# Low parts of attention's second weight pair: from VectorE's norm to GpSimd

## The chip, the cores and the metric

The kernel runs on one core of one Trainium2 chip (trn2). The metric is the device time of one execution in microseconds (us). Three runs of the kernel before gave 2669.30, 2670.77 and 2672.90 us, a median of 2670.77 us. The time of the kernel after is compared with it.

## What is computed

Two model blocks stand one behind the other, on a sequence of 512 positions and a width of 1024, all in 32-bit floats. The first has an S5 state-space mixer, a feed-forward layer, a short convolution and another feed-forward layer, and ends with `rms_norm(x, final_g)`. The second has dilated window attention, a feed-forward layer, an HGRN2 mixer and a last feed-forward layer. The stretch of this study lies between the two:

```
    return rms_norm(x, final_g)                     # end of the first block
...
    proj = (x @ w_in).reshape(B, S, N_GROUPS, 3, ATTN_HEADS, ATTN_HEAD_DIM)
    # start of dilated_attention_mixer: w_in is 1024 x 9216
```

`rms_norm` divides each position's 1024 numbers by the root of their mean square and multiplies by a gain; attention projects the result with `w_in` to queries, keys and values.

## The kernel before, in words

**Split products.** A product of 32-bit accuracy is made of three passes of TensorE over reduced operands. Each operand is the sum of a high part (rounded to the type fp32r) and a low part (operand less high part). Activations stand as `Hh` and `Hl`, or `Gh` and `Gl`; weights as `Wh` and `Wl`, and in attention as `WhA` and `WlA`. A tile is `Wh*Hl + Wl*Hh + Wh*Hh`, three matmuls for each of eight slices k of the contraction.

**The weight stream.** Weights come as `pairs`, numbered by p; each pair has two halves h. SP loads half h of pair p from HBM into `raw[:, h]`; ScalarE casts it to the high part (`split_half`, L1169 to L1177, or `split`) and raises `split_h`; VectorE subtracts, giving the low part (`low_half`, L1613 to L1616, or `low`), and raises `split_l`. `raw` has one buffer for each half, so SP's load of pair p waits for `split_l >= 2p - 1 + h` (L472): the low part of the same half of the pair before must be done. TensorE waits for `split_l >= 2p + 2` before it uses pair p. In attention a half is 128 x 1536; there are 24 pairs from P_ATTN on, in two buffers (`wa[p % 2]`).

**The norm in front of attention** is number 4. Its input X is complete only when the last product of the feed-forward layer is (`last_product`), and it is done in two halves of 256 columns (positions), so that TensorE can start on the first half while the second is normed. For each half VectorE adds the squares, TensorE sums them over partitions, ScalarE takes a first estimate of the reciprocal root, VectorE betters it in three steps (`newton`, L1624 to L1626), and then for each slice k VectorE multiplies (`scaled`, L1968), ScalarE casts to `Hh` (L1192) and VectorE subtracts to `Hl` (`lowp`, L2009), raising `nm_l`. TensorE's first three attention tiles (L808 to L810) take slice k of a half as soon as its `nm_l` is there: nine matmuls of 256 columns for each k and half, 72 for a half. Only then do the next tiles (L800 to L802, from pair P_ATTN + 1) follow.

**The order around the change** is written out by hand in each engine's program. ScalarE (`norm`, L1204 to L1221) casts half 0 of pair P_ATTN + 1 behind slices 4 and 5 of the first half, then makes the estimate for the second half, casts slices 6 and 7, and then casts half 1 of the pair. VectorE (`last_down`, L2042 to L2102) ends the first half's slices 6 and 7, computes the low part of half 0 of pair P_ATTN + 1, and only then does the three `newton` steps of the second half (`rstd_end`). It does slices 0 to 3 of the second half, computes the low part of the pair's half 1, and does slices 4 to 7.

GpSimd works at the start (tables of the state-space mixer, L2463 to L2532) and issues 42 loads for the modulation weights, the last 40 each behind a wait for VectorE's use of the buffer (L2546 to L2548). It has nothing behind them in its program.

Of the kernel before, what the change touches and what calls it, by code (L numbers as in the profile page):

```python
# [17 lines left out]
F32 = mybir.dt.float32  # L18
# [31 lines left out]
P_ATTN = P_FFN_B + 17  # L50
# [29 lines left out]
def half(h):  # L80
    return slice(h * H2, (h + 1) * H2)
# [7 lines left out]
def tiles_done(n, k, h):  # L89

    f = first_halved(n)
    before = 0 if n == 1 else 10 + 12 * (n - 2)
    return before + (k + 1 if k < f else f + h * (KT - f) + k - f + 1)
# [26 lines left out]
def half_width(p):  # L120

    if P_CONV <= p < P_CONVO:
        return (4 * 384, 4 * 384)
    if P_ATTN <= p < P_ATTNO:
        return (4 * 384, 4 * 384)
    if P_HGRN <= p < P_HGRNO:
        return (2048, 2048) if p in (P_HGRN, P_HGRNO - 1) else (1024, 1024)
    if p in (P_FFN_A + 15, P_FFN_A + 16, P_FFN_B + 15, P_FFN_B + 16):
        return (2048, 1024)
    return (2048, 2048)  # L130


def build(nc, xT, xU, cT, cC, adap, adaw, bada, norms, s5a, s5bc, s5d, wstream, convw, lnp, hgn, lbl,
          rot, masks, hmask, consts, jsel, gsel, out):
    with ExitStack() as ctx:
        masks = masks.bitcast(BF16)

        def sem(name):
            return ctx.enter_context(nc.semaphore(name))

        def sb(name, shape, dt=F32, c=ctx):
            return c.enter_context(nc.sbuf_tensor(name, shape, dt))
# [20 lines left out]
        raw = sb("raw", [P, 2, HALF])  # L163
# [119 lines left out]
        ada2_used, c2_in, c2_act = sem("ada2_used"), sem("c2_in"), sem("c2_act")  # L283
        split_h = sem("split_h")
        split_l = sem("split_l")
        acc_ready = sem("acc_ready")
        free_act = sem("free_act")
        free_dve = sem("free_dve")
# [20 lines left out]
        class Order:  # L309
# [4 lines left out]
            def step(self, ins):  # L314
                ins.then_inc(self.s, 1)
                self.n += 1

            def sync(self):
                self.eng.wait_ge(self.s, self.n)

            def link(self, ins):
                self.step(ins)
                self.sync()
# [41 lines left out]
        def w_high(p, h, n):  # L365
            return w_part(Wh, WhA, p, h, n)

        def w_low(p, h, n):
            return w_part(Wl, WlA, p, h, n)
# [1230 lines left out]
        def _(dve):  # L1600
# [12 lines left out]
            def low_half(p, h):  # L1613
                dve.wait_ge(split_h, 2 * p + h + 1)
                w = half_width(p)[h]
                TT(w_low(p, h, w), raw[:, h, 0:w], w_high(p, h, w).bitcast(F32), ALU.subtract).then_inc(split_l, 1)  # L1616

            def ahead(p):
                if p + 1 < N_PAIRS:
                    low(p + 1, half_width(p + 1))  # L1620
# [12 lines left out]
            n, r, q, m, s = pr[12], pr[13], pr[14], pr[15], pr[7]  # L1633
# [238 lines left out]
            def add_square(n, k, h=0):  # L1872

                f = first_halved(n)
                c = slice(0, T) if k < f else half(h)
                dve.wait_ge(nm_sq, squares_done(n, k, h))
                if k > 1:
                    dve.wait_ge(nm_sa, square_adds_done(n, k - 1, h))
                TT(SQA[:, c], SQA[:, c], sq[:, k % 2, c], ALU.add).then_inc(nm_sa, 1)

            for j in range(4):
                p = P_SSM + j
# [76 lines left out]
            def scaled(n, k, h):  # L1959
                gain, bias, eps = NORM[n]  # L1960
                c = half(h)
                t = tmp[:, k % 4, c]
                if n in LN_INDEX:
                    if k >= AHEAD:
                        link(TT(t, X[:, k, c], mu[:, c], ALU.subtract))
                    STT(t, t, gain(k), Rn[:, c], ALU.mult, ALU.mult).then_inc(nm_t, 1)
                elif bias is None:
                    STT(X[:, k, c], X[:, k, c], gain(k), Rn[:, c], ALU.mult, ALU.mult).then_inc(nm_t, 1)  # L1968
                else:
                    STT(t, X[:, k, c], gain(k), Rn[:, c], ALU.mult, ALU.mult).then_inc(nm_t, 1)  # L1970

            def last_pair(k):

                c = half(0)
                t = tmp[:, k % 4:k % 4 + 2, c]
                if k >= 4:
                    dve.wait_ge(nm_l, normed_done(8, k - 3, 0))
                    link(TT(t, X[:, k:k + 2, c], twice(mu[:, c]), ALU.subtract))
                TT(t, t, twice(Rn[:, c]), ALU.mult).then_inc(nm_t, 2)
# [23 lines left out]
            def lowp(n, k, h):  # L2003
                gain, bias, eps = NORM[n]
                c = half(h)
                hh = Hh[:, k, :].bitcast(F32)
                dve.wait_ge(nm_h, normed_done(n, k, h))
                if bias is None:
                    TT(class_half(Hl[:, k, :], h), X[:, k, c].rearrange("p (n r) -> p n r", r=4), class_half(hh, h), ALU.subtract).then_inc(nm_l, 1)  # L2009
                else:  # L2010
                    STT(Hl[:, k, c], tmp[:, k % 4, c], bias(k), hh[:, c], ALU.add, ALU.subtract).then_inc(nm_l, 1)

            def normed(n, h, ks):

                for k in ks:
                    if n == 8:
                        if k % 2 == 0:
                            last_pair(k)
                        continue
                    if k == 0:  # L2020
                        scaled(n, 0, h)
                    if k + 1 < KT:
                        scaled(n, k + 1, h)
                    lowp(n, k, h)
# [17 lines left out]
            def last_down(p, n, add):  # L2042

                ln = LN_INDEX.get(n)

                def tiles(k, h):
                    c = half(h)
                    if k == 6 and h == 1:
                        add_square(n, 4, 1)
                        add_square(n, 5, 1)  # L2050
                    if k == 4 and h == 0:
                        for x in range(1, 4):
                            add_square(n, x)
                    if h:
                        dve.wait_ge(acc_ready, 4 * p + k - 2)
                    else:
                        dve.wait_ge(acc_half, 2 * (n - 1) + k // 2 - 1)
                    add(k, PS[:, 4 * (p % 2) + 2 * h + k // 2 - 2, :].rearrange("p (m n) -> p m n", m=2), c)
                    if ln is not None:
                        for x in (k, k + 1) if k == 4 else (k,):  # L2060
                            dve.wait_ge(nm_x, tiles_done(n, x, h))
                            sync()
                            ins = TT(nv[:, 0, c], nv[:, 0, c], X[:, x, c], ALU.add)
                            if n == 8 and h == 1 and x == KT - 2:
                                link(ins)
                                STT(nv[:, 0, c], nv[:, 0, c], -1.0, X[:, KT - 1, c], ALU.mult, ALU.subtract).then_inc(nm_xs, 1)
                            elif x < KT - 2:
                                step(ins)
                            else:
                                ins.then_inc(nm_xs, 1)  # L2070
                    if k == 4 and h == 0:
                        add_square(n, 4, 0)
                        add_square(n, 5, 0)
                    if k == 6:
                        add_square(n, 6, h)

                ahead(p)
                tiles(4, 0)
                tiles(6, 0)
                rstd(n, 0)  # L2080
                normed(n, 0, (0, 1))
                tiles(4, 1)
                normed(n, 0, (2, 3))
                tiles(6, 1)
                dve.wait_ge(nm_x, tiles_done(n, 7, 1))
                dve.sem_inc(free_dve, 1)
                if n == 4:
                    normed(n, 0, (4, 5))
                    rstd(n, 1, early=True)
                    normed(n, 0, (6, 7))  # L2090
                    low_half(P_ATTN + 1, 0)
                    rstd_end(n, 1)
                else:
                    normed(n, 0, range(4, KT))
                    if n == 8:
                        last_half()
                        return
                    rstd(n, 1)
                normed(n, 1, range(4))
                if n == 4:  # L2100
                    low_half(P_ATTN + 1, 1)
                normed(n, 1, range(4, KT))  # L2102

            hc = [10, 0]

# [123 lines left out]
            for j in range(8):  # L2229
                p = P_CONV + j  # L2230
# [68 lines left out]
            for un in range(8):  # L2299
                p = P_ATTN + 3 * un  # L2300
# [140 lines left out]
        def _(pool):  # L2441
# [103 lines left out]
            for a in range(len(ADA2)):  # L2545
                if a >= 2:  # L2546
                    pool.wait_ge(ada2_used, a - 1)
                pool.dma_start(adab[:, a % 2, :], adaw[ADA2[a] - N_ADA_PE]).then_inc(ada2_in[a % 2], 16)  # L2548


def layout(x, c, norm1_g, norm2_g, w_ada, b_ada, ssm_a_re, ssm_a_im, ssm_log_step, ssm_b_re, ssm_b_im, ssm_c_re, ssm_c_im,
           ssm_d, ssm_w_out, conv_w_in, conv_w, conv_w_out, w_ffn_in, w_ffn_out, final_g, attn_w_in_2, attn_w_out_2,
# [156 lines left out]
```

## Time and profile before

| what | value |
|---|---|
| median of three runs | 2670.77 us |
| the profiled execution's own time | 2671.11 us |
| its span | 2669.3 us |
| VectorE busy | 1467.4 us, 55% |
| ScalarE busy | 1050.7 us, 39% |
| GpSimd busy | 116.7 us, 4% |
| mean granted clock of TensorE | 0.994 of full speed |

A busy time is the sum of an engine's instructions; overlaps between engines aren't taken out. The span is the profiled part of the execution; 1.8 us of the execution lie around it. All times inside the trace count from the start of the span.

### The profile page before, as it was taken

To read this page: it belongs to the slowest core of one execution; us is meant where nothing else is said; L and a number is where in the kernel's file an instruction comes from. 1 tells how busy PE (TensorE), PEld (TensorE's weight loads), DVE (VectorE), ACT (ScalarE), POOL (GpSimd) and SP (SyncE) were. 2 spreads that over 40 slices of the span, in tenths; PEclk is the share of its full clock that TensorE was granted. 3 is DMA by queue.
4 is the path that set the end of the run, shared out by engine and by line. 5 is a ranking of instruction groups with operands and counts; after the bars stand their busy time and mean duration, and the time that the engine had idled before them with its cause. 6 is when DMAs were issued, how large, how long until landed. Compare 5 with 4: busy or idle time off the path is not lost.

```text
span 2669.3 us, 38086 instructions
## 1 busy us (share of the span) xinstructions
PE 2625.1 (98%) x15920; PEld 2217.9 (83%) x15920; DVE 1467.4 (55%) x2173; ACT 1050.7 (39%) x1495; POOL 116.7 (4%) x150
## 2 busy tenths in 40 slices
PE   6999999999999999999999999999999999999998
PEld 3689888888898888888888888988888988988887
DVE  8967555565563333465555555744336777833335
ACT  4535222233242222355555555523223665522323
POOL 7610000000000000000000000000000000000000
PEclk8999999999999999999999999999999999999999
DMA  6084555422322322222222222132222222232220
GB/s 244 2 307 169 194 190 189 181 72 95 111 95 97 104 103 100 87 72 77 79 72 72 78 78 81 56 125 95 95 95 80 60 84 95 80 111 95 95 95 32
DMA packets 46246, 282.89 MB, mean 106 GB/s; under 512 B 6129, under 2 KB 8561, under 8 KB 20098
## 3 DMA queue, kind: packets, MB, share of 16 engines
q1 hardware_dynamic: 40146, 238.02, 26.1%
q0 software_dynamic: 5936, 42.51, 4.2%
q8 instruction: 125, 2.05, 0.3%
q14 instruction: 39, 0.32, 0.0%
HBM read 278.41 MB, written 2.10 MB: 105 GB/s over the span
## 4 chain that ended last, share of the span: by engine, by line
PE 89%; DVE 7%; ACT 3%; DMA 1%; issue 1%; SPq 0%; DVEq 0%; ACTq 0%
PE PS L665 18%; PE PS L666 18%; PE PS L667 18%; PE PS L800 4%; PE PS L802 4%; PE PS L801 4%; PE PS L889 2%; PE PS L757 1%; PE PS L758 1%; PE PS L756 1%; PE PS L637 1%; PE PS L829 1%; PE PS L830 1%; PE PS L831 1%; PE PS L877 1%; PE PS L691 1%
## 5 line engine op out<-in xcount | busy, mean ns | idle before, releaser
L665 PE MATMUL PS<-Hl,Wh 128*128 128x512 f32 x1256 | 489.1, 389 | 0.8 <-DVE Wl L1611 0.7
L666 PE MATMUL PS<-Hh,Wl 128*128 128x512 f32 x1256 | 488.7, 389 | 0.0
L667 PE MATMUL PS<-Hh,Wh 128*128 128x512 f32 x1256 | 488.7, 389 | 0.0
L1167 ACT CAST Wh<-raw 128x2048 fp32r<-128x2048 f32 (+2 forms) x156 | 281.3, 1848 | 400.5 <-PE PS L667 380.3
L1611 DVE TENSOR_TENSOR Wl<-raw,Wh 128x2048 fp32r<-128x2048 f32 (+2 forms) x160 | 347.0, 2207 | 67.0 <-ACT Wh L1167 66.8
L665 PE MATMUL PS<-Gl,Wh 128*128 128x512 f32 x880 | 342.5, 389 | 0.0
L666 PE MATMUL PS<-Gh,Wl 128*128 128x512 f32 x880 | 342.4, 389 | 0.0
L667 PE MATMUL PS<-Gh,Wh 128*128 128x512 f32 x880 | 342.4, 389 | 0.0
L665 PEld LDWEIGHTS PS<-Hl,Wh 128*128 128x128 f32 x1256 | 235.8, 188 | 50.1 <-DVE Wl L1611 1.4
L667 PEld LDWEIGHTS PS<-Hh,Wh 128*128 128x128 f32 x1256 | 235.8, 188 | 49.1
L666 PEld LDWEIGHTS PS<-Hh,Wl 128*128 128x128 f32 x1256 | 235.8, 188 | 48.6
L667 PEld LDWEIGHTS PS<-Gh,Wh 128*128 128x128 f32 x880 | 165.2, 188 | 34.4
L665 PEld LDWEIGHTS PS<-Gl,Wh 128*128 128x128 f32 x880 | 165.2, 188 | 34.3
L666 PEld LDWEIGHTS PS<-Gh,Wl 128*128 128x128 f32 x880 | 165.2, 188 | 34.1
L1365 ACT ACTIVATE tmp<-PS 128x512 f32<-128x512 f32 x108 | 64.6, 598 | 314.4 <-PE PS L667 311.6
L800 PE MATMUL PS<-Hl,WhA 128*128 128x512 f32 x424 | 170.2, 402 | 0.0
L802 PE MATMUL PS<-Hh,WhA 128*128 128x512 f32 x424 | 165.6, 391 | 0.0
L801 PE MATMUL PS<-Hh,WlA 128*128 128x512 f32 x424 | 165.3, 390 | 0.0
L2116 DVE TENSOR_TENSOR tmp<-PS,tmp 128x512 f32<-128x512 f32 x44 | 30.4, 691 | 244.9 <-PE PS L667 240.2
L1371 ACT CAST Gh<-tmp 128x512 fp32r<-128x512 f32 x108 | 62.8, 620 | 216.7 <-DVE tmp L2116 214.4
L756 PE MATMUL PS<-Gl,Wh 128*128 128x256 f32 x480 | 137.3, 286 | 0.0
L2213 DVE TENSOR_TENSOR tmp<-tmp 128x512 f32<-128x512 f32 x64 | 43.6, 690 | 169.6 <-ACT tmp L1365 169.6
(460 smaller groups left out, 4790.5 us busy)
## 6 DMA issues: line engine op xcount, KB each, us to landing
raw<-wstream SPq DMA_DIRECT2D x152, 1024.0 KB, 6.5
raw<-wstream SPq DMA_DIRECT2D x64, 768.0 KB, 4.5
adab<-adaw POOLq DMA_DIRECT2D x40, 1024.0 KB, 5.7
raw<-wstream SPq DMA_DIRECT2D x20, 512.0 KB, 3.7
raw<-adap SPq DMA_DIRECT2D x4, 1024.0 KB, 11.2
ada_land<-adap SPq DMA_DIRECT2D x4, 1024.0 KB, 19.2
X<-xT SPq DMA_DIRECT2D x1, 2048.0 KB, 8.7
XU<-xU SPq DMA_DIRECT2D x1, 1536.0 KB, 15.3
```

Source lines behind the costliest of these rows:

```text
L665: mm(o, Wh[:, s, c0:c0 + P], xl[:, k, :], start=k == 0, stop=False)
L666: mm(o, Wl[:, s, c0:c0 + P], xh[:, k, :], start=False, stop=False)
L667: last = mm(o, Wh[:, s, c0:c0 + P], xh[:, k, :], start=False, stop=k == kt - 1)
L756: mm(o, Wh[:, s, c0:c0 + P], Gl[:, k, c], start=k == 0, stop=False)
L800: mm(o, WhA[p % 2][:, c0:c0 + P], Hl[:, k, :], start=k == 0, stop=False)
L801: mm(o, WlA[p % 2][:, c0:c0 + P], Hh[:, k, :], start=False, stop=False)
L802: return mm(o, WhA[p % 2][:, c0:c0 + P], Hh[:, k, :], start=False, stop=k == KT - 1)
L889: return mm(PS[64 * h:64 * h + 64, 7 if (un, r) == (7, 3) else 6, r * P + lo:r * P + hi], v[:, 64 * h:64 * h + 64], PT[h][:, j * P + lo:j ...
L1167: nc.scalar.copy(w_high(p, h, widths[h]), raw[:, h, 0:widths[h]]).then_inc(split_h, 1)
L1365: A(tmp[:, t % 4, :], PS[:, 4 * (p % 2) + m, :], func).then_inc(hid_t, 1)
L1371: nc.scalar.copy(Gh[:, g0 + m, :], tmp[:, t % 4, :]).then_inc(hid_h, 1)
L1611: TT(w_low(p, h, widths[h]), raw[:, h, 0:widths[h]], w, ALU.subtract).then_inc(split_l, 1)
```

## The change

GpSimd computes the two low parts of pair P_ATTN + 1. It raises a new semaphore `split_p`. VectorE no longer computes them; it waits for `split_p` and raises `split_l` itself, for half 0 behind slices 0 to 3 of the second half of the norm, and for half 1 behind slices 4 to 7.

```diff
+        split_p = sem("split_p")
...
                     normed(n, 0, (6, 7))
-                    low_half(P_ATTN + 1, 0)
                     rstd_end(n, 1)
...
                 normed(n, 1, range(4))
                 if n == 4:
-                    low_half(P_ATTN + 1, 1)
+                    dve.wait_ge(split_p, 1)
+                    dve.sem_inc(split_l, 1)
                 normed(n, 1, range(4, KT))
+                if n == 4:
+                    dve.wait_ge(split_p, 2)
+                    dve.sem_inc(split_l, 1)
...
                 pool.dma_start(adab[:, a % 2, :], adaw[ADA2[a] - N_ADA_PE]).then_inc(ada2_in[a % 2], 16)
+
+            for h in range(2):
+                p = P_ATTN + 1
+                w = half_width(p)[h]
+                pool.wait_ge(split_h, 2 * p + h + 1)
+                TTg(w_low(p, h, w), raw[:, h, 0:w], w_high(p, h, w).bitcast(F32), ALU.subtract).then_inc(split_p, 1)
```

`TTg` is GpSimd's `tensor_tensor`. The operands and the result are those of the removed instructions.

## Rows read from the trace of the kernel before

**Rows 1.** The page: busy time of TensorE, and the chain that ended last
```profile
PE 2625.1 (98%) x15920; PEld 2217.9 (83%) x15920; DVE 1467.4 (55%) x2173; ACT 1050.7 (39%) x1495; POOL 116.7 (4%) x150
...
PE 89%; DVE 7%; ACT 3%; DMA 1%; issue 1%; SPq 0%; DVEq 0%; ACTq 0%
```

**Rows 2.** Waits of TensorE, whole run: us in total, times, longest us
```profile
PE PS L808 <- DVE Hl L2009: 3.8, 2, 2.9
```

**Rows 3.** Timeline of TensorE in norm 4: start, us, instruction, idle before
```profile
1143.01 0.39 PE L808 MATMUL PS<-Hl,WhA 128*128 128x256 f32 x1 [0.91 <-DVE Hl L2009]
...
1145.14 0.28 PE L810 MATMUL PS<-Hh,WhA 128*128 128x256 f32 x1
1148.28 0.58 PE L808 MATMUL PS<-Hl,WhA 128*128 128x256 f32 x1 [2.85 <-DVE Hl L2009]
...
1154.19 0.28 PE L808 MATMUL PS<-Hl,WhA 128*128 128x256 f32 x1
...
1159.59 0.40 PE L800 MATMUL PS<-Hl,WhA 128*128 128x512 f32 x1
```

**Rows 4.** Stretches: length, TensorE busy (instructions), granted clock, DMA share, GB/s
```profile
1148.00:1150.00 2.00, 1.72 (x8) 0.50 0.46 190
```

**Rows 5.** Timeline of VectorE, same stretch
```profile
1140.80 0.48 DVE L1968 SCALAR_TENSOR_TENSOR X<-X,NRM,Rn 128x256 f32<-128x256 f32 x1
1142.35 1.15 DVE L2009 TENSOR_TENSOR Hl<-X,Hh 128x256 fp32r<-128x256 f32 x2 [1.06 <-ACT Hh L1192]
1143.40 1.75 DVE L1616 TENSOR_TENSOR WlA<-raw,WhA 128x1536 fp32r<-128x1536 f32 x1
1145.07 0.42 DVE L1624 TENSOR_TENSOR nv<-Rn 128x256 f32<-128x256 f32 x1
...
1147.62 0.60 DVE L2009 TENSOR_TENSOR Hl<-X,Hh 128x256 fp32r<-128x256 f32 x1 [0.30 <-ACT Hh L1192]
...
1150.90 1.75 DVE L1616 TENSOR_TENSOR WlA<-raw,WhA 128x1536 fp32r<-128x1536 f32 x1
```

**Rows 6.** Timeline of ScalarE: the two casts of pair P_ATTN + 1, and the next pair's
```profile
1139.38 1.50 ACT L1177 CAST WhA<-raw 128x1536 fp32r<-128x1536 f32 x1
...
1142.56 1.48 ACT L1177 CAST WhA<-raw 128x1536 fp32r<-128x1536 f32 x1
...
1166.19 1.49 ACT L1177 CAST WhA<-raw 128x1536 fp32r<-128x1536 f32 x1
```

**Rows 7.** Timeline of GpSimd: two inputs of three sizes, VectorE not in its way
```profile
21.87 0.46 POOL L2471 TENSOR_TENSOR AP_<-etmp 128x128 f32<-128x128 f32 x1
...
25.64 0.66 POOL L2471 TENSOR_TENSOR QP<-etmp 128x224 f32<-128x224 f32 x1
...
41.19 1.27 POOL L2532 TENSOR_TENSOR Et<-etmp 128x512 f32<-128x512 f32 x1
```

**Rows 8.** Timeline of VectorE while GpSimd works
```profile
27.09 1.59 DVE L1770 TENSOR_TENSOR rt<-QP,BC 128x512 f32<-128x512 f32 x1
28.71 0.69 DVE L1774 TENSOR_TENSOR Ft<-PS,rt 128x512 f32<-128x512 f32 x1
...
36.13 1.26 DVE L1769 TENSOR_TENSOR PS<-QP,BC 128x512 f32<-128x512 f32 x1
37.31 1.75 DVE L1770 TENSOR_TENSOR rt<-QP,BC 128x512 f32<-128x512 f32 x1
```

**Rows 9.** Timeline of GpSimd in the same two stretches
```profile
26.48 1.65 POOL L2506 TENSOR_TENSOR ftmp<-QP,BC 128x512 f32<-128x512 f32 x1 [0.18 <-POOL QP L2471]
28.21 1.43 POOL L2507 TENSOR_TENSOR ftmp<-QP,BC 128x512 f32<-128x512 f32 x1
...
35.78 1.06 POOL L2525 TENSOR_TENSOR etmp<-AP_,BC 128x512 f32<-128x512 f32 x1
36.92 1.59 POOL L2529 TENSOR_TENSOR Et<-etmp 128x512 f32<-128x512 f32 x1
```

**Rows 10.** Weight loads: SP's queue in norm 4, and us from issue to landing
```profile
1145.32 62.54 SPq L473 DMA_DIRECT2D raw<-wstream  x8
```
```profile
raw<-wstream SPq DMA_DIRECT2D x64, 768.0 KB, 4.5
```

## The prediction

> **What bounds the kernel now.** I began with the page. TensorE is busy for 98% of the span, and the chain that ended last is 89% TensorE [rows 1], so time is lost or won only where TensorE stands still. Next I read whom it waits for: in norm 4 it waits for VectorE's `Hl`, 3.8 us in two waits [rows 2]. The timeline of TensorE places them. It is 0.91 us idle before slice 6 of the first half. After slice 7, whose last matmul begins at 1145.14, it is 2.85 us idle until slice 0 of the second half at 1148.28 [rows 3]. The wait has an aftermath: the granted clock is then 0.50, which is 1.2 GHz [rows 4]. The 27 matmuls from 1148.28 to 1154.19 take 5.91 us; the other 45 of the half, from 1154.19 to 1159.59, take 5.40 us, or 0.120 us each at 2.4 GHz. At that rate 27 would take 3.24 us, so the low clock costs 2.67 us.
>
> The timeline of VectorE says why TensorE waits. Its two `Hl` of slices 6 and 7 end at 1143.50. The low part of weight half 0 fills 1143.40 to 1145.07, where `newton` begins, and the first `Hl` of the second half ends at 1147.62 + 0.60 = 1148.22 [rows 5]. The removed instruction thus lies on the path for 1145.07 - 1143.40 = 1.67 us. From the start of `newton` to that `Hl` are 3.15 us. The other low part, at 1150.90, costs TensorE nothing now: it works on slices 0 to 3 until about 1155.
>
> **Part 1: two instructions leave VectorE.** By itself, the first brings `newton` and TensorE's restart forward by 1.67 us. The second shortens VectorE's queue by as much, but slice 4 waits for nothing in it while TensorE is at the low clock, so I take 0. If the clock stayed high, slice 4 would be wanted 36 matmuls, 4.3 us, behind slice 0, and the low part would start to show; its removal then keeps that cover.
>
> **Part 2: the same work on GpSimd.** With two inputs it takes 0.46 us for 128 columns, 0.66 for 224 and 1.27 for 512 [rows 7]. That is (1.27 - 0.46) / 384 = 0.0021 us a column. For 1536 columns: 1.27 + 1024 x 0.0021 = 3.43 us each, 6.9 us for both. No row shows GpSimd writing fp32r. As bounds I take VectorE's 1.67 us below and, above, twice the reckoned 3.43; I choose 3.43, since the removed instruction shows VectorE's own pace unchanged by that type. GpSimd can begin when ScalarE's casts end, at 1139.38 + 1.50 = 1140.88 and 1142.56 + 1.48 = 1144.04 [rows 6].
>
> **Part 3: what it does to VectorE.** This term decides. While GpSimd works early in the kernel, VectorE's instructions with both inputs in SBUF are held up: 1.59 us, 1.26 and 1.75 for 128x512. The one that takes an input from PSUM, at 28.71, runs in its 0.69 us [rows 8]. The ends fit a hold until GpSimd is done. GpSimd's instruction of 26.48 ends at 28.13, and VectorE's of 27.09 ends at 28.68, 0.55 us later; GpSimd's of 35.78 ends at 36.84, and VectorE's of 36.13 ends at 37.39, again 0.55 us later. GpSimd is held up in turn, 1.43 against 1.06 us [rows 9]. And they take turns: GpSimd, waiting since 36.92, runs before VectorE's instruction of 37.31, which ends only at 39.06. The Trainium skill, SBUF — State Buffer, section "SBUF: two separate sides", says that a VectorE instruction with two SBUF inputs and a GpSimd one lock a shared port pair, and that whichever starts first keeps it for its whole length. The trace agrees, with the 0.55 us above; by this rule alone the sum is the one below, and were it left aside, it would be rival A's.
>
> In norm 4 `scaled` (X and Rn), `lowp` (X or Hh) and `newton` all read two SBUF tensors [rows 5]. So I lay the two GpSimd instructions into VectorE's line:
> - the first starts when VectorE's `scaled` of 1140.80 is off the port, about 1141.2, and ends at about 1144.6. `Hl` of slice 6, due at 1142.35, ends at about 1145.1 instead of shortly before 1143.01, when TensorE took it [rows 3]. VectorE was idle for 1.06 us in that time anyway [rows 5], which hides that much;
> - the second has been ready since its cast ended at 1144.04. By the turns it goes next: 1145.1 to 1148.5. `Hl` of slice 7 ends 0.55 us later, 1149.05, instead of 1143.50;
> - `newton` starts at about 1149.0 and the first `Hl` of the second half is there 3.15 us later, at 1152.15 instead of 1148.22: 3.9 us late.
>
> The same by balance: 6.9 us of GpSimd, less 1.1 hidden, less 1.67 removed, less about 0.2 of rounding at the turns, gives 3.9. If VectorE kept the port for several instructions, or GpSimd took it twice running, both would still lie ahead of that `Hl`, and the sum would hold. TensorE's slices 6 and 7 are late too, but that is inside the 3.9: it finishes slice 7 at about 1150 or 1151, before 1152.
>
> **Part 4: the second half of the norm.** No GpSimd instruction is left, so VectorE delivers a slice every 0.93 us as before, without the second low part. TensorE takes its 72 matmuls as before, 11.3 us, if the clock is low for about as long (below). The first attention tile of pair P_ATTN + 1 starts 3.9 us late, and everything behind it is moved by as much.
>
> **Part 5: signals and loads.** The new waits cost 0: `split_p` reaches 2 at 1148.5, and VectorE gets to the first wait at about 1155, to the second at about 1158.7. Behind them stand slices 4 to 7, SP's loads of pair P_ATTN + 2, and TensorE's tile 3 (wanted at about 1163.5). The loads are issued at about 1155 and 1158.7 instead of 1145.32 and 1152.6, and land 4.5 us later [rows 10], so by 1163.5; the cast that wants the first was at 1166.19 [rows 6] and moves to about 1170. Cover: some 10 us for the first, and as much for the second. SP has nothing urgent queued behind. GpSimd's queue holds only loads of the modulation weights, long issued. If a load did come late, the cast of pair P_ATTN + 2 would be late first.
>
> **The clock.** The low clock began after idle time of 2.85 us and lasted until 1154.19. In the new order TensorE is idle about 3.3 us, works 1.1, is idle 2.7, works 1.1 to 1.9 and is idle 1 to 2, so I expect the low clock again. How long it lasts from the restart on isn't fixed by a row: bounds are no slow matmul (2.7 us won) and all 72 slow (45 x 0.099 = 4.4 us more, at 5.91 / 27 = 0.219 against 0.120 us). I take the 27 of before, the only row of its kind.
>
> **Sum:** -1.67 (removed) + 6.9 - 1.1 - 0.2 = +3.9 us. Against the profiled execution's own 2671.11 us that is 2675.0; it stood 0.3 us above the median, so for a median 2670.77 + 3.9 = **2674.7 us**, 0.15% slower. A measurement of this kernel can tell about 0.2%, 5.3 us, from no change.
>
> **Rivals.**
> *A. No hold (12%).* VectorE is not held by so plain a stream, say because the lock was met in rows with 512 columns only. Then the restart is at 1146.6, the idle time 1.2 us, close to the 0.91 that left the clock high [rows 3]: -1.67 - 2.67 = -4.3 us, 2666.5. With the low clock all the same: 2669.1. Against it stand three held instructions and none of the kind that went free.
> *B. Slower: the low clock stays for the whole half (13%).* Three idle times in 11 us instead of one, and all 72 matmuls at 0.219 us: 3.9 + 4.4 = 8.3, 2679.1. It decides from 15 further slow matmuls on (15 x 0.099 = 1.5 us above my sum). For it: more idle time than before. Against it: after the restart TensorE is as busy as before, and then the clock rose after 27.
> *C. Slower: fp32r costs GpSimd more (7%).* At twice the length the sum is 3.9 + 6.9 = 10.8, 2681.6; it passes 5.3 us when one instruction takes over 4.15 us.
> *D. Only one of the two holds VectorE on the path (6%).* The second finds its turn in idle stretches: 3.9 - 3.4 = 0.5 us, 2671.3. `newton` and ScalarE leave gaps of only 0.3 us, which speaks against it.
> *E. The edit does nothing (2%)*, for instance as the low parts cost VectorE nothing either way: 2670.8. The 1.67 us on the path speak against it.
>
> **The numbers.** The forecast has 60%, with its own range of 2672.5 to 2677. For 8 in 10 I go down to 2669.0, which takes in D, E and the low-clock end of A, and up to 2680.0, which takes in B; A's 2666.5 and most of C stay out. Slower by over 0.2%: B, C and a small part of the forecast, 0.22. Faster by over 0.2% needs more than A's full gain: 0.04. Within: 0.74.
>
> **What would show it.** Right: GpSimd's two new instructions at 3.4 us, the first at about 1141; `Hl` of slices 6 and 7 at about 1145 and 1149 with long durations; a restart of TensorE near 1152; granted clock 0.50 behind it. Wrong: `lowp` and `newton` at their old durations beside GpSimd, or a restart before 1148.3. GpSimd at 6 us would be C; no return of the clock by 1159, B.

## The result, and the profile after

The kernel after takes 2675.65 us (median of 17 runs, 2673.46 to 2677.94), the kernel before 2670.61 us (17 runs, 2669.09 to 2673.87). The ratio is 1.0016 with a 95% interval of 1.0009 to 1.0022: 5.0 us slower by the medians, 2.4 to 5.9 us by the interval. The forecast was 3.9 us.

First the page of the kernel after: the span, busy times, and TensorE's granted clock in 40 slices.

```profile
span 2673.7 us, 38088 instructions
...
PE 2627.2 (98%) x15920; PEld 2219.5 (83%) x15920; DVE 1469.5 (55%) x2171; ACT 1050.7 (39%) x1495; POOL 124.2 (5%) x152
...
PEclk8999999999999999989999999999999999999999
```

VectorE has two instructions less and is busy for 2.1 us more. GpSimd has two instructions more and is busy for 7.5 us more [rows 1]. That is the first sign: VectorE lost two instructions that took 1.67 us each from one start to the next, and its busy time still rose. The timelines of GpSimd and of VectorE in norm 4, where lines stand one to four lower than before, show where:

```profile
1141.69 7.40 POOL L2558 TENSOR_TENSOR WlA<-raw,WhA 128x1536 fp32r<-128x1536 f32 x2 [621.68 <-ACT WhA L1178]
```
```profile
1141.54 0.47 DVE L1969 SCALAR_TENSOR_TENSOR X<-X,NRM,Rn 128x256 f32<-128x256 f32 x1
1143.08 6.46 DVE L2010 TENSOR_TENSOR Hl<-X,Hh 128x256 fp32r<-128x256 f32 x2 [1.07 <-ACT Hh L1193]
1149.46 0.41 DVE L1625 TENSOR_TENSOR nv<-Rn 128x256 f32<-128x256 f32 x1
...
1152.02 0.60 DVE L2010 TENSOR_TENSOR Hl<-X,Hh 128x256 fp32r<-128x256 f32 x1 [0.31 <-ACT Hh L1193]
```

The two `Hl` of slices 6 and 7 took 1.15 us together [rows 5] and now take 6.46. In that time GpSimd's two subtractions run. `newton` begins when they are over, and the rest of VectorE's chain has its old durations. TensorE follows:

```profile
1145.84 0.58 PE L809 MATMUL PS<-Hl,WhA 128*128 128x256 f32 x1 [3.00 <-DVE Hl L2010]
...
1149.60 0.58 PE L809 MATMUL PS<-Hl,WhA 128*128 128x256 f32 x1 [1.47 <-DVE Hl L2010]
...
1152.68 0.58 PE L809 MATMUL PS<-Hl,WhA 128*128 128x256 f32 x1 [0.79 <-DVE Hl L2010]
...
1163.93 0.40 PE L801 MATMUL PS<-Hl,WhA 128*128 128x512 f32 x1
```

One idle time of 0.91 us and one of 2.85 [rows 3] have become 3.00, 1.47 and 0.79 us. Slices 6 and 7 now run between them at the low clock: 0.50 was granted from 1145.90 to 1148.00 and from 1149.60 to 1151.40, where slice 6 had run at the high clock before.

**A measure for the stage.** Absolute times differ between executions for a reason ahead of this stage (below). So I count from the start of VectorE's multiplication of slice 7 of the first half, the last thing ahead of GpSimd's work (1140.80 before, 1141.54 after). The *restart* is TensorE's first matmul on the second half; the *stage* ends with its first matmul of pair P_ATTN + 1. Before: restart 1148.28 - 1140.80 = 7.48, stage 1159.59 - 1140.80 = 18.79 [rows 3, 5]. After: 11.14 and 22.39. The restart is 3.66 us later, the stage 3.60 us longer. Behind the stage nothing differs: from its end to the end of the span are 1509.7 us before and 1509.8 after.

### The profile page after: what moved, and what is told of

Read it like the earlier page. It is cut to its first block, busy times and chain, and to the rows that moved or that the text cites. A ratio compares the mean times of both kernels' runs of the same rounds, so it can differ in the third digit from the quotient of the medians.

```text
span 2673.7 us, 38088 instructions
## 1 busy us (share of the span) xinstructions
PE 2627.2 (98%) x15920; PEld 2219.5 (83%) x15920; DVE 1469.5 (55%) x2171; ACT 1050.7 (39%) x1495; POOL 124.2 (5%) x152
## 3 DMA queue, kind: packets, MB, share of 16 engines
q1 hardware_dynamic: 40146, 238.02, 25.8%
## 4 chain that ended last, share of the span: by engine, by line
PE 87%; DVE 8%; ACT 3%; DMA 2%; issue 1%; DVEq 0%; ACTq 0%; SPq 0%
PE PS L666 17%; PE PS L668 17%; PE PS L667 17%; PE PS L801 4%; PE PS L803 4%; PE PS L802 4%; PE PS L890 2%; PE PS L759 1%; PE PS L758 1%; PE PS L757 1%; PE PS L830 1%; PE PS L831 1%; PE PS L832 1%; PE PS L638 1%; PE PS L878 1%; DVE Wl L1612 1%
```

## The experiments

Twelve runs were made, two of them repeats of the kernels before and after. The table has each one's restart and stage in us, the "slow" matmuls (those of the 72 of the second half with over 0.18 us from their start to the next), and, where the kernel was timed, its median and that of before, timed along with it. A wait behind a matmul counts as slow too, and so does the first matmul behind a wait, which takes 0.22 us or more at either clock. So 1 or 2 in this column mean that no matmul ran at the low clock, and of the 6 of half 0 only, timed, four did.

| kernel | restart | stage | slow | median, and before's |
|---|---|---|---|---|
| before | 7.48 | 18.79 | 27 | 2670.61 |
| before again | 7.47 | 17.55 | 14 | |
| after | 11.14 | 22.39 | 26 | 2675.65; 2670.61 |
| after again | 11.13 | 21.69 | 19 | |
| early signal | 11.38 | 22.07 | 20 | 2675.54; 2670.69 |
| GpSimd writes only | 5.82 | 14.56 | 1 | |
| GpSimd copies | 7.07 | 17.31 | 16 | |
| half 0 only | 8.06 | 17.72 | 2 | |
| half 0 only, timed | 7.92 | 17.71 | 6 | 2671.51; 2670.86 |
| half 1 only | 10.70 | 21.71 | 24 | |
| half 1 twice | 14.39 | 25.31 | 23 | 2678.82; 2670.69 |
| GpSimd behind the norm | 5.80 | 19.27 | 2 | 2674.78; 2670.86 |
| VectorE, both at the end | 5.80 | 15.55 | 2 | 2668.55; 2670.69 |
| VectorE, gap and end | 6.33 | 15.07 | 1 | 2667.99; 2670.69 |

### What holds VectorE: reads, or any GpSimd work

Two kernels change only what GpSimd does with the same buffers. Both leave the low parts out, so they do less than the kernel needs and serve the timelines alone:

```diff
-                TTg(w_low(p, h, w), raw[:, h, 0:w], w_high(p, h, w).bitcast(F32), ALU.subtract).then_inc(split_p, 1)
+                g_.memset(w_low(p, h, w).bitcast(F32), 0.0).then_inc(split_p, 1)
```

> GpSimd only writes zeros to the two low parts, so the low parts of pair P_ATTN + 1 are left out. The stage is the time from VectorE's multiplication of slice 7 of the first half (L1968 before, L1969 after) to TensorE's first matmul of pair P_ATTN + 1: 18.79 us before, 22.39 after. Theory (GpSimd's SBUF reads hold VectorE's instructions with two SBUF inputs): nothing is read, nothing is held, Hl of slices 6 and 7 keep their 0.6 us, the restart comes 1.67 us earlier than before, and the clock may stay high: stage 14.5 to 17.1. Rival (any GpSimd work beside the norm slows VectorE, reads or not): Hl of slices 6 or 7 takes over 1 us and the stage is above 18.8.

and, in place of the memset,

```diff
+                g_.tensor_copy(w_low(p, h, w), raw[:, h, 0:w]).then_inc(split_p, 1)
```

> GpSimd copies raw into the low parts, one SBUF input in place of two; the subtraction is left out. Theory (hold for the length of any GpSimd instruction that reads SBUF): Hl of slice 6 and of slice 7 each end about 0.5 us behind a copy; the hold is as long as the copies are, so the stage is below the 22.39 us of the kernel after by twice the difference of a copy from 3.43 us. Rival (only GpSimd's two-input instructions hold): no long Hl, stage 14.5 to 17.1 as in the memset run.

GpSimd and VectorE in the run that only writes:

```profile
1144.51 1.38 POOL L2558 MEMSET WlA<- 128x1536 f32 x1 [621.67 <-ACT WhA L1178]
1147.68 1.38 POOL L2558 MEMSET WlA<- 128x1536 f32 x1 [1.79 <-ACT WhA L1178]
```
```profile
1145.94 1.15 DVE L2010 TENSOR_TENSOR Hl<-X,Hh 128x256 fp32r<-128x256 f32 x2 [1.07 <-ACT Hh L1193]
1146.99 0.42 DVE L1625 TENSOR_TENSOR nv<-Rn 128x256 f32<-128x256 f32 x1
1147.45 0.43 DVE L1626 SCALAR_TENSOR_TENSOR nv<-nv 128x256 f32<-128x256 f32 x1
1147.91 0.42 DVE L1627 SCALAR_TENSOR_TENSOR Rn<-nv,Rn 128x256 f32<-128x256 f32 x1
1148.37 0.88 DVE L1969 SCALAR_TENSOR_TENSOR X<-X,NRM,Rn 128x256 f32<-128x256 f32 x2
```

The second memset covers 1147.68 to 1149.06, and the last step of `newton` (two SBUF inputs) and the multiplications start in it and keep their plain durations. No hold; the restart is 1.66 us earlier than before, the whole removed instruction. The run that copies:

```profile
1142.09 1.69 POOL L2558 CAST WlA<-raw 128x1536 fp32r<-128x1536 f32 x1 [621.64 <-ACT WhA L1178]
1145.29 1.59 POOL L2558 CAST WlA<-raw 128x1536 fp32r<-128x1536 f32 x1 [1.52 <-ACT WhA L1178]
```
```profile
1145.13 0.42 DVE L1626 SCALAR_TENSOR_TENSOR nv<-nv 128x256 f32<-128x256 f32 x1
1145.59 1.57 DVE L1627 SCALAR_TENSOR_TENSOR Rn<-nv,Rn 128x256 f32<-128x256 f32 x1
```

The second copy ends at 1146.88; the step of `newton` issued at 1145.59 ends at 1147.16, 0.28 us later, after 1.57 us instead of 0.42. So one read input is enough to hold. The step before it, at 1145.13, had begun ahead of the copy and was not held. My expectation named `Hl` of both slices as the ones held, which was wrong in detail: the first copy was over at 1143.78, when the `Hl` issued at 1143.53 had hardly begun to wait, and the pair took 1.25 us. A short GpSimd instruction lay almost wholly in VectorE's idle time. The stage missed its number for the same reason: two copies that each held for their length would have given 22.39 less about 3.6, or 18.8 us, and it was 17.31.

The Trainium skill, SBUF — State Buffer, section "SBUF: two separate sides", has the lock apply against a two-input VectorE instruction "only against a GpSimd op that reads SBUF". The memset and the copy agree.

### Whether the price adds up by the instruction

Half 0 alone on GpSimd, half 1 on VectorE at its old place; and the other way round:

```diff
-            for h in range(2):
+            for h in range(1):
...
+                    low_half(P_ATTN + 1, 1)
```

> GpSimd computes half 0 alone, VectorE half 1 at its old place behind slices 0 to 3. Theory (the hold adds up by the instruction, 3.4 us each less 1.07 hidden by VectorE's idle time): newton starts at 3.43 - 1.07 - 1.67 + 0.1 = 0.8 us later than before, stage about 19.3 to 19.8. Rival (most of the loss comes from the second waiting, from signals or from loads): stage as after, 22.4, or as before, 18.8.

> GpSimd computes half 1 alone, VectorE half 0 at its old place ahead of newton. Theory (turns): GpSimd is ready at the end of the second cast, gets the port when VectorE's low part of half 0 ends, and holds newton for 3.4 us, with nothing hidden: stage 18.79 + 3.4 = 22.1 or a little more, about what both cost. Rival (each instruction costs half of the 3.6 us): stage 20.6.

VectorE with half 0 only, and then with half 1 only:

```profile
1144.35 3.23 DVE L2010 TENSOR_TENSOR Hl<-X,Hh 128x256 fp32r<-128x256 f32 x2 [1.07 <-ACT Hh L1193]
1147.49 0.42 DVE L1625 TENSOR_TENSOR nv<-Rn 128x256 f32<-128x256 f32 x1
```
```profile
1145.64 1.76 DVE L1617 TENSOR_TENSOR WlA<-raw,WhA 128x1536 fp32r<-128x1536 f32 x1
1147.31 3.66 DVE L1625 TENSOR_TENSOR nv<-Rn 128x256 f32<-128x256 f32 x1
```

With half 1 only, GpSimd began to wait at 1146.37 while VectorE had the port, got it next, and held the first step of `newton` for 3.66 us instead of 0.42. The restart is 3.22 us later than before. With half 0 only, `newton` starts 0.41 us later than before, counted in the stage, where 0.8 was expected, and the restart is 0.58 us later. A part of this 0.58 isn't VectorE's: TensorE, on slices 6 and 7 at the low clock, came to the second half without idle time, after its `Hl` was there. In the second profile of this kernel TensorE did wait for that `Hl`, and the restart was 0.44 us later than before. With 3.22 that adds to 3.66, which is what the kernel after has. So the price isn't half and half. The second costs 3.2 us because nothing hides it and it takes nothing off the path; the first costs 0.4 to 0.6 because VectorE's idle time and the removed 1.67 us stand against it.

The *stage* of half 0 only missed its number, 17.72 against 19.3 to 19.8, because of the clock; that has a part of its own below. With half 1 only it was 21.71 against "22.1 or a little more", with 24 slow matmuls in place of 27.

Then a price doubled: GpSimd subtracts half 1 twice.

```diff
+                if h == 1:
+                    link(TTg(w_low(p, h, w), raw[:, h, 0:w], w_high(p, h, w).bitcast(F32), ALU.subtract))
```

> The kernel after, with GpSimd's subtraction of half 1 done twice. Theory (each GpSimd instruction holds VectorE for its length when it gets its turn): the additional one falls between newton's steps or slices of the second half and costs 3.4 us more: stage 25.8, 8.4 us above before. Rival (the hold is bounded, or comes from the signals): stage 22.4 to 23.

```profile
1142.65 6.47 DVE L2010 TENSOR_TENSOR Hl<-X,Hh 128x256 fp32r<-128x256 f32 x2 [1.06 <-ACT Hh L1193]
1149.04 3.67 DVE L1625 TENSOR_TENSOR nv<-Rn 128x256 f32<-128x256 f32 x1
```

The third instruction holds the first step of `newton`, and the restart is 3.25 us later than in the kernel after. The stage is 25.31 us where 25.8 was expected, with 23 slow matmuls in place of 26. The median, 8.1 us above before, fits the expected 8.4.

### Whether the moved signals or loads cost anything

VectorE's two waits and signals directly behind `newton` of the second half:

```diff
                     rstd_end(n, 1)
+                    dve.wait_ge(split_p, 2)
+                    dve.sem_inc(split_l, 1)
+                    dve.sem_inc(split_l, 1)
```

> The kernel after with VectorE's two waits and signals directly behind newton of the second half, so that both loads of pair P_ATTN + 2 are issued at about 1151 instead of 1154.85 and 1158.9. Theory (the loads have slack, the hold is the cost): time as after, 5 us above before, stage 22.4. Rival (moved signals and loads cost the 1.3 us that the median shows beyond my sum): 1 to 1.5 us less than after.

The median is 2675.54 us, 4.9 us above before (ratio 1.0019, interval 1.0010 to 1.0028), that of the kernel after to 0.1 us. The restart is 0.24 us later, as the signals now stand between `newton` and the first multiplication, which waits 0.28 us. Both loads are issued from 1150.57 us on. The kernel after issues its first load at 1154.85 us; the cast that wants it comes at 1170.53:

```profile
1154.85 57.34 SPq L474 DMA_DIRECT2D raw<-wstream  x8
```
```profile
1170.53 1.48 ACT L1178 CAST WhA<-raw 128x1536 fp32r<-128x1536 f32 x1
```

It has no idle time in front of it: ScalarE's own work leads up to it, not the load. The stage came out at 22.07 us, where 22.4 was expected. No price of the late signals or loads shows.

### GpSimd behind the norm

```diff
                 pool.wait_ge(split_h, 2 * p + h + 1)
+                pool.wait_ge(nm_l, normed_done(4, 7, 1))
```

VectorE passes both signals on behind slice 7.

> The kernel after, with GpSimd also waiting for the last Hl of the second half, so that its work is behind the norm and not beside it. Theory: VectorE's norm is held by nothing, TensorE restarts 5.8 us behind the multiplication of slice 7 (the runs without a hold: 5.80 and 5.82), the last Hl is there at about 12.4 us, GpSimd needs 7.2 us from there, and TensorE waits some 5 us for pair P_ATTN + 1: stage about 19.7, 0.9 us above before, and up to 3 us more behind it if the clock falls in that wait. Rival (the hold is not the cause, and GpSimd's place does not matter): restart at about 11 us, as in the kernel after.

```profile
1155.04 6.85 POOL L2557 TENSOR_TENSOR WlA<-raw,WhA 128x1536 fp32r<-128x1536 f32 x2 [633.86 <-DVE Hl L2010]
```
```profile
1162.00 0.80 PE L801 MATMUL PS<-Hl,WhA 128*128 128x512 f32 x1 [4.59 <-DVEq L2104]
1163.44 0.63 PE L801 MATMUL PS<-Hl,WhA 128*128 128x512 f32 x1
```

The norm runs free: the restart is at 5.80. Here GpSimd's instruction is seen undisturbed: 6.85 / 2 = 3.43 us, the value reckoned from narrower ones. TensorE then waits 4.59 us for the pair, and afterwards runs at 1.2 GHz for a while (granted clock 0.50 from 1162 to 1164 us, 0.69 to 1166, then 1.00). The stage is 19.27 us where about 19.7 was expected, 0.5 us longer than in the first profile of before and 1.7 us longer than in the second, and 1.5 us more go behind it: 1511.3 us from its end to the end of the span instead of 1509.8. The median is 3.9 us above before (ratio 1.0013, interval 1.0004 to 1.0023); the stage and what lies behind it make 2.0 us of that against the first profile, 3.2 against the second. Beside the norm GpSimd holds VectorE; behind it it's too slow by itself.

### Both low parts on VectorE, but off the path

> VectorE computes both low parts itself, behind slice 7 of the second half; GpSimd does nothing. Theory (no hold; 1.67 us off the path, no low clock, 2.67 us; TensorE then waits about 1.2 us for the low parts): stage 15.6 to 16.2, 2.5 to 3.2 us faster than before. Rival (the low clock comes back all the same): 17.1 and no wait at the end, 1.7 us faster than before.

```diff
-                    low_half(P_ATTN + 1, 0)
                     rstd_end(n, 1)
...
-                if n == 4:
-                    low_half(P_ATTN + 1, 1)
                 normed(n, 1, range(4, KT))
+                if n == 4:
+                    low_half(P_ATTN + 1, 0)
+                    low_half(P_ATTN + 1, 1)
```

> VectorE computes both low parts, half 0 in its 1.07 us of idle time between the multiplication of slice 7 and Hl of slice 6, half 1 behind slice 7 of the second half. Theory: newton starts 1.0 us earlier than before, TensorE's idle time falls from 2.85 to about 1.9 us less 0.6 that goes to slice 6; if the clock stays high, stage about 15.1, 3.6 us faster than before; if not, 17.8, 1.0 us faster.

```diff
-                    normed(n, 0, (6, 7))
+                    scaled(n, 7, 0)
                     low_half(P_ATTN + 1, 0)
+                    lowp(n, 6, 0)
+                    lowp(n, 7, 0)
                     rstd_end(n, 1)
```

with half 1 behind slice 7 of the second half. VectorE and TensorE in that kernel:

```profile
1142.39 1.75 DVE L1616 TENSOR_TENSOR WlA<-raw,WhA 128x1536 fp32r<-128x1536 f32 x1
1144.06 1.15 DVE L2009 TENSOR_TENSOR Hl<-X,Hh 128x256 fp32r<-128x256 f32 x2
```
```profile
1144.72 0.39 PE L808 MATMUL PS<-Hl,WhA 128*128 128x256 f32 x1 [1.44 <-DVE Hl L2009]
...
1148.33 0.39 PE L808 MATMUL PS<-Hl,WhA 128*128 128x256 f32 x1 [1.19 <-DVE Hl L2009]
```

The low part takes the place of the 1.07 us in which VectorE waited for ScalarE, and the clock stays high. The medians are 2668.55 us, ratio 0.9993 (0.9984 to 1.0002), for both at the end, and 2667.99 us, ratio 0.9990 (0.9981 to 0.9999), for gap and end. By its interval, which ends close to 1, the second is faster than before, by 2.7 us in the medians; for the first that isn't settled. Stages came as forecast (15.55 for 15.6 to 16.2, 15.07 for 15.1), the gains in the medians 0.4 to 1 us smaller. That fits the stage of before, whose first profile was at the dear end (next).

### The clock from execution to execution

The last three runs repeat kernels.

> The kernel before once more, for a second profile. If the low clock of the stage depends on more than the program, the restart stays at 7.5 us behind the multiplication of slice 7 within 0.1, and the number of slow matmuls moves (27 in the first profile) and with it the stage of 18.79 us. If the program alone fixes it, 27 again.

> The kernel after once more. Restart at 11.1 us within 0.1; slow matmuls 26 in the first profile, 20 in the run with early signals: between these if the clock moves by itself, stage 21.6 to 22.5.

> Half 0 alone on GpSimd, timed. The profile had the restart at 8.06 us (before: 7.48), but only 2 slow matmuls behind it against 27, and a stage of 17.72. If that clock is the rule for this order, it is about 1 us faster than before; if it was chance, about 0.6 us slower, with 20 slow matmuls or more in the new profile.

Restarts repeat to 0.01 us in before and after; the number of slow matmuls doesn't: 27 and 14 before, 26 and 19 after (20 to 26 had been expected), so the stage of before is 18.79 or 17.55 us and that of after 22.39 or 21.69. Half 0 only had no matmul of the 72 at the low clock in one profile and four in the other, although TensorE had been idle for 3.02 us before slice 6 in both. Two stretches of the first, the untimed run, show where the clock came back:

```profile
1150.00:1151.00 1.00, 1.00 (x8) 0.63 0.00 0
1151.00:1152.00 1.00, 1.00 (x11) 1.00 0.00 0
```

There TensorE resumed at 1147.12 us with slices 6 and 7 at the low clock, had the high clock back at about 1150.7, and went straight on into the second half at 1150.87. At that rate VectorE's low part of half 1 did show, as the prediction had it for a clock that stays high: TensorE was 0.77 us idle before slice 4. Timed, the kernel is 0.7 us above before in the medians (ratio 1.0001, 0.9992 to 1.0010): no difference. Neither branch of the expectation came: the kernel isn't 1 us faster, and the second profile has the short stage again (17.71) and not 20 slow matmuls. The "1 us faster" had been reckoned from the first profile of before; against the second profile the stage is no shorter. Why the low clock ended there some 3.6 us after TensorE had resumed, while in the kernel after, with idle times of 1.47 and 0.79 us between, it lasted into the second half, the runs don't settle.

The repeated kernel before was in its stage 1.24 us shorter and in its span 2.9 us longer, 2672.2. Its stage began 4.03 us later, at 1144.83 us. The waits of TensorE between 203 and 257 us, in the first and in the second profile of before, have a part of it:

```profile
PE PS L524 <- DVE nv L1879: 0.8, 1, 0.8
```
```profile
PE PS L524 <- DVE nv L1879: 3.2, 1, 3.2
```

In the second profile VectorE's wait for a load of modulation weights (L1866) ended at 201.19 us instead of 198.69, its sums behind it ended at 212.6 instead of 210.1, and the clock was low between 220 and 224 us. In the first it was never low there. By 256 us the second execution was 4.0 us behind, and it was still 4.03 us behind in norm 4. So the difference of these two executions ahead of the stage arose by norm 1. Whether the spread of 4.8 us over the 17 runs of before has the same source isn't shown.

## Why the prediction was right

**The rows that decided.** [rows 8, 9], from 1100 us ahead of the change, had the price: VectorE's two-input instructions wait for GpSimd's whole instruction. All three held durations were of 128x512; the hold proved the same against 1536 columns.

**Term by term.**
- Removed, -1.67: the restart without any hold is 1.66 and 1.68 us earlier than before.
- GpSimd's two, 6.9: 6.85 us undisturbed. Beside the norm they span 7.40, with VectorE's turn between them.
- Hidden, -1.1: VectorE's idle time was 1.07.
- Sum for the restart, +3.9: measured 3.66. The `Hl` of slice 6 let TensorE start at 4.30 in the stage instead of 2.21, 2.1 us later, as worked out; `newton` began 3.65 us later than before, counted in the stage (7.92 against 4.27), where the sum had 3.9. A further turn cost 3.24 us (half 1 only) and 3.25 (half 1 twice) and not 3.43: the held step of `newton` ends 0.28 us behind GpSimd's instruction, and its own length is 0.42.
- Signals and loads, 0: shown by the early signals.
- Clock, "the 27 of before": 26 and 19 came, but 27 itself was one draw, and 14 the next, so that 26 came so near it was luck. The two profiles of before average 18.17 us for the stage, the two of after 22.04: +3.9. One profile of each would not have told this term to better than a microsecond.

**What is left.** The medians differ by 5.0 us, the stages by 3.6 to 3.9. The rest is inside the interval (2.4 to 5.9), and no place for it was found: behind the stage the profiles agree to 0.1 us, and ahead of it executions of one kernel differ by 4 us. The clock is a candidate: of the 17 runs of after, the four with a mean granted clock of 0.992 took 2677.6 us in the median and the four with 0.994 took 2674.1, and the two profiled executions had 0.993. No run separates it, so it stays unresolved: the forecast accounts for the restart, and some 1 us of the 5.0 is explained by nothing here.

**The rivals.** A (no hold) fell with the 6.46 us of two `Hl`. What A would have brought is real, though: with GpSimd only writing, the stage is 14.56, 4.2 us shorter than the 18.79 of before, where A had 4.3. B (low clock for the whole half) fell: 26 and 19 of 72. C (fp32r dearer) fell with 3.43 us. D (one of the two costs nothing) is false for the second, which costs 3.2, but close for the first, 0.4 to 0.6. E fell with the interval, 2.4 to 5.9 us slower.

## What to carry to other kernels

Before work is moved from VectorE to GpSimd, look at what VectorE does at that time: instructions with two SBUF inputs stand still for the whole of a GpSimd instruction that reads SBUF, so the move replaces 1.67 us by 3.43 on the same line. Look for VectorE's own idle time, and for a place behind the point that another engine waits for: the same two subtractions in that order gave 2.7 us where GpSimd had cost 5. And where the clock of TensorE may fall in a stage, compare restarts, which repeated to 0.01 us in the kernels before and after, rather than stages or single spans; where the low clock makes TensorE itself the last to be ready, as in half 0 only, look at the instruction that it waits for.

## What the runs showed of the hardware that was not expected

A GpSimd copy of 128x1536 with one input took 1.59 to 1.69 us and a memset 1.38, against 3.43 for the subtraction with two inputs, over twice the copy. When VectorE and GpSimd both had work queued, they took turns: GpSimd's subtraction, waiting since 1146.37 us in the run with half 1 only, went ahead of VectorE's next instruction. TensorE's clock, where it had been high, stayed high behind idle times of 0.90 to 1.44 us before slices of this norm. Behind one of 2.33 us (GpSimd copies), of 2.85 (before) and of 6.09 (half 1 only) the second half started at the low clock, for 14 to 27 of its 72 matmuls, and the number differed by 13 between two executions of the kernel before. Behind 3.00 to 3.02 us before slice 6, the slice's nine matmuls ran at the high clock in some profiles (early signal, half 1 twice, half 0 only timed) and eight or more of them at the low one in others (the first profiles of after and of half 0 only).
